# A two-block transformer kernel: weight splits of the delta net taken apart, and the end of each delta-net half reordered with the keys ahead of the queries

## Chip, cores and metric

The kernel runs on one core of a Trainium2 chip. The metric is device time in microseconds for one execution. PE is TensorE, DVE is VectorE, ACT is ScalarE, POOL is GpSimd, SP the queue engine that issues most DMAs.

## What is computed

Two transformer blocks follow each other on x of shape (1, 512, 1024), all in float32. The first has a differential attention, a gated delta net that runs forward and backward, a merge of both, and an expert-choice feed-forward layer with 16 experts; the second has a band attention, an RWKV layer and a feed-forward layer. The change lies in the first block alone. Its delta net, cut to what matters:

```python
qkv_g = jax.nn.silu(centred_depthwise_conv(qkv_g, conv_w[l]))      # 5 taps
qg, kg, vg = jnp.split(qkv_g, [GDN_QK, 2 * GDN_QK], axis=-1)        # 8 heads of 128
qg = l2norm(qg...); kg = l2norm(kg...)
g_f = -exp(a_log_fwd) * softplus(a_f + dt_bias_fwd)                 # and g_b
beta_f = sigmoid(b_f)                                               # and beta_b
# gated_delta_rule_chunked, forward and on flipped inputs:
q = chunks(q) * dk ** -0.5
g = jnp.cumsum(chunks(g), axis=-1)
decay = where(incl, exp(g_i - g_j), 0)
a_mat = where(strict, (k_beta @ k.T) * decay, 0)
sol = triangular_solve(a_mat + I, [v * beta, k_beta * exp(g)])
qk = where(incl, (q @ k.T) * decay, 0)
# then a scan over the chunks: o = q_dec @ S + qk @ v_new, S updated
```

## The kernel before

Everything is one program written out by hand for five engines that meet through counted semaphores. Each engine works strictly in the order written. Weights of the projections come through a ring of three slots. A weight tile is split into a rounded high part (`split_act`, L481, on ACT, 128x2048) and the remainder (`split_pool`, L489, on POOL, in place); PE then makes three products per 128 rows (L570 to L572). Split number k may be written once the tile of number k-2 has been used.

**Attention.** `attention_pe` projects queries, keys and values (L591 to L593), `attention_act` copies the value tiles out (L769). Between value projection and scores lie the small computations of the decays: ACT's L775, L776 and L778 (exponentials on 128x64) and DVE's L876 to L886. DVE's `maxima` (L892) reads the scores (L683), ACT's L785 makes the exponentials. At the end DVE scales the heads (L927), PE turns them (L727, `heads_out_pe`, behind the first delta-net tile), and ACT copies them (L822).

**Delta net.** It works in two halves of four heads (`gr` 0 and 1), each with three phases.

1. `group_*`: twelve feature tiles (4 queries, 4 keys, 4 values) are projected. Per tile ACT copies the projection twice (L1266 and, as the middle tap, L1274), DVE adds the other four taps (L1322) and forms the silu (L1309) with ACT's tanh (L1285), PE turns the tile to tokens (L1219), ACT copies it (L1288), POOL squares it (L1349) and DVE sums the squares (L1304). From tile 6 on ACT also makes one exponential of the decay matrices `DE` per tile (L1294, four instructions). After tile 11 come Ln and Exp of the norms (L1278, L1280), each with a table load. DVE scales eight token tiles (L1337), PE turns them back (L1253) into banks 4 and 5 by turns, ACT copies them (L1298).
2. `heads_*`: eight Gram products on PE (L1363: four key by key into banks 0 to 3, four key by query into banks 4 to 7). DVE multiplies the key products with the decays of each direction into `PT` (L1419), POOL multiplies these by beta (L1446), ACT copies the query products (L1392), POOL multiplies them by the decays (L1450). ACT copies the 16x16 corners of `PT` (L1095, eight per direction, named lanes f and b) into `C32`; DVE adds the two halves (L1135). Then the triangular systems are inverted: row matmuls (L1008), a chain of DVE steps (L1147, L1150), a widening (L1156), and so on. POOL makes masked copies `LT` (L1201).
3. `scan_*`: four chunks in each direction.

PE's waits at the end of a half, in its own order:

```python
            pe.wait_ge(*count("iv_sel", gr + 1))
            pe.wait_ge(*count("gd_pt", 8 * (gr + 1)))
            pe.wait_ge(*count("gd_qk", HG * (gr + 1)))
            for p in range(7 + 2):
                if p < 8:
                    inv_rows_pe(pe, f, gr, sel, p)
                if p >= 2:
                    inv_rows_pe(pe, b, gr, sel, p - 2)
```

## Time and profile before

| | |
|---|---|
| median of 3 runs | 2964.2 us (2950.64 to 2964.31) |
| profiled execution | 2965.58 us, span 2963.4 us |
| busy: PE, DVE, ACT, POOL | 90%, 31%, 26%, 20% |
| mean granted TensorE clock | 0.959 of 2.4 GHz |
| chain that ended last | PE 70%, DMA 12%, DVE 9%, ACT 5% |

The granted clock is 1.00 (2.4 GHz) or 0.50 (1.2 GHz) at any moment, and a mean over a stretch says how much of it was at either. In a timeline a row gives start, duration (of all instructions of the row), engine, line, operation, output and input, shape and count; in brackets stands how long the engine was idle ahead of it and what ended that. A matmul of float32 operands is shown as two instructions, a transpose as one.

### The profile page before, as it was taken

The page shows a single profiled execution, that of the slowest core. Times are in us where ns is not written, and L with a number is a line of the kernel's source. Part 1 is how long each engine was busy: PE and PEld are TensorE (multiplying, and loading weights), DVE is VectorE, ACT ScalarE, POOL GpSimd, SP SyncE. Part 2 cuts the span into 40 slices and gives each one's busy share as a digit, 9 for nine tenths or more (in the row PEclk, how much of TensorE's full clock was granted, in tenths as well). Part 3 has the DMA queues.
Part 4 walks back from the last instruction along what each step waited for, and adds up shares of the span by engine and source line. Part 5 has one row for each costly group of instructions (what it writes and reads, how often), then busy time and mean ns, then how long its engine had stood idle before and what let it go on. Part 6 is the DMA issues. An engine that isn't in the chain of part 4 may idle for free.

```text
span 2963.4 us, 34221 instructions
## 1 busy us (share of the span) xinstructions
PE 2661.8 (90%) x14439; PEld 1739.9 (59%) x14439; DVE 911.3 (31%) x1604; ACT 759.9 (26%) x1290; POOL 582.3 (20%) x173
## 2 busy tenths in 40 slices
PE   7989978879999999888988898888878899999998
PEld 5756767768566743323323333356657766788886
DVE  2348655654111311011011110123565521241221
ACT  3247643532111110000100100043342121431222
POOL 3310452452113000000000000022211122244442
PEclk9999979979999999999999999999988999999999
DMA  4300312203224699999999999943100032322322
GB/s 143 114 29 1 114 58 86 72 15 114 85 85 155 261 383 428 427 429 428 429 429 428 428 429 428 428 150 114 50 14 1 16 114 93 121 91 87 100 100 71
DMA packets 130852, 559.36 MB, mean 189 GB/s; under 512 B 7256, under 2 KB 88480, under 8 KB 103080
## 3 DMA queue, kind: packets, MB, share of 16 engines
q1 hardware_dynamic: 129864, 551.28, 46.8%
q0 software_dynamic: 864, 6.29, 0.5%
q8 instruction: 95, 1.56, 0.2%
q14 instruction: 29, 0.24, 0.0%
HBM read 547.01 MB, written 10.54 MB: 188 GB/s over the span
## 4 chain that ended last, share of the span: by engine, by line
PE 70%; DMA 12%; DVE 9%; ACT 5%; issue 2%; POOL 0%; DVEq 0%; SPq 0%; ACTq 0%; POOLq 0%
DMA S<-in_w_up 11%; PE PS L570 8%; PE PS L572 8%; PE PS L571 8%; PE PS L2101 7%; PE PS L2068 7%; PE PS L560 4%; PE PS L2051 2%; PE PS L3217 2%; PE PS L3219 2%; PE PS L3220 2%; PE PS L3064 2%; PE PS L2112 1%; DMA S<-in_w_down 1%; PE PS L548 1%
## 5 line engine op out<-in xcount | busy, mean ns | idle before, releaser
L2363 POOL TENSOR_TENSOR r_block<-S,r_block 128x2048 fp32r<-128x2048 f32 x57 | 261.5, 4588 | 1488.3 <-ACT r_block L2352 1479.5
L2068 PE MATMUL PS<-S 128*64 128x512 f32 x2048 | 458.3, 598 | 72.3 <-DMA S<-in_w_up 68.8
L570 PE MATMUL PS<-r_block,r_block 128*128 128x512 f32 x1040 | 417.8, 402 | 3.2 <-POOL r_block L2363 2.0
L572 PE MATMUL PS<-r_block,r_block 128*128 128x512 f32 x1040 | 405.3, 390 | 0.0
L571 PE MATMUL PS<-r_block,r_block 128*128 128x512 f32 x1040 | 404.8, 389 | 0.0
L2068 PEld LDWEIGHTS PS<-S 128*64 128x64 f32 x2048 | 141.3, 137 | 380.1 <-issue 248.4
L489 POOL TENSOR_TENSOR r_block<-S,r_block 128x2048 fp32r<-128x2048 f32 x40 | 183.1, 4578 | 565.4 <-ACT r_block L481 457.2
L2101 PE MATMUL PS<-S 128*64 128x512 f32 x1024 | 225.6, 597 | 5.8 <-DMA S<-in_w_down 2.5
L570 PEld LDWEIGHTS PS<-r_block,r_block 128*128 128x128 f32 x1040 | 195.3, 188 | 49.6 <-issue 8.0
L571 PEld LDWEIGHTS PS<-r_block,r_block 128*128 128x128 f32 x1040 | 195.4, 188 | 45.0 <-issue 6.0
L572 PEld LDWEIGHTS PS<-r_block,r_block 128*128 128x128 f32 x1040 | 195.2, 188 | 41.4
L2235 DVE SCALAR_TENSOR_TENSOR S<-S,PS 128x512 f32<-128x512 f32 x32 | 22.0, 688 | 486.2 <-ACT S L2163 462.8
L2101 PEld LDWEIGHTS PS<-S 128*64 128x64 f32 x1024 | 75.8, 138 | 144.7 <-issue 139.9
L2352 ACT ACTIVATE r_block<-S 128x2048 fp32r<-128x2048 f32 x57 | 108.9, 1912 | 171.8 <-PE PS L3220 117.6
L560 PE MATMUL PS<-S 128*128 128x512 f32 x256 | 110.5, 592 | 0.0
L3217 PE MATMUL PS<-r_block,r_block 128*128 128x512 f32 x256 | 99.8, 390 | 1.4 <-ACT S L3236 1.4
L481 ACT ACTIVATE r_block<-S 128x2048 fp32r<-128x2048 f32 x40 | 76.4, 1913 | 95.8 <-DMA S<-in_w_in 68.2
L2242 DVE TENSOR_TENSOR S<-S,PS 128x512 f32<-128x512 f32 x32 | 20.6, 684 | 258.6 <-PE PS L2068 258.6
L3219 PE MATMUL PS<-r_block,r_block 128*128 128x512 f32 x256 | 99.6, 389 | 0.0
L3220 PE MATMUL PS<-r_block,r_block 128*128 128x512 f32 x256 | 99.6, 389 | 0.0
L3259 DVE TENSOR_TENSOR S<-S 128x512 f32<-128x512 f32 x32 | 37.9, 1185 | 188.7 <-ACT S L3236 188.7
L1322 DVE SCALAR_TENSOR_TENSOR PS<-S,PS 128x512 f32<-128x512 f32 x96 | 72.5, 756 | 44.3 <-ACT PS L1274 41.7
(455 smaller groups left out, 3686.4 us busy)
## 6 DMA issues: line engine op xcount, KB each, us to landing
S<-in_w_gate SPq DMA_DIRECT2D x64, 2048.0 KB, 17.9
S<-in_w_up SPq DMA_DIRECT2D x64, 2048.0 KB, 21.0
S<-in_w_down SPq DMA_DIRECT2D x64, 2048.0 KB, 25.6
S<-in_w_in SPq DMA_DIRECT2D x57, 1024.0 KB, 5.1
S<-in_w_up SPq DMA_DIRECT2D x16, 1024.0 KB, 5.3
S<-in_w_down SPq DMA_DIRECT2D x16, 1024.0 KB, 4.8
S<-decay_rows SPq DMA_DIRECT2D x8, 1024.0 KB, 6.7
S<-in_w_out SPq DMA_DIRECT2D x8, 1024.0 KB, 4.9
```

The source lines that it names most:

```text
L489: pool.tensor_tensor(r32(w), w, rounded(WH[k % 2]), ALU.subtract).then_inc(sem("w_low"), 1)
L560: mm = pe.matmul(out, w[:, dc, off:off + P], src[:, dc, :], start=(dc == 0), stop=(dc == DC - 1))
L570: pe.matmul(out, wh, r32(HT[:, dc, :]), start=(dc == 0), stop=False)
L571: pe.matmul(out, wh, r32(low[:, dc, :]), start=False, stop=False)
L572: mm = pe.matmul(out, wl, r32(HT[:, dc, :]), start=False, stop=(dc == DC - 1))
L2068: mm = pe.matmul(PS[c * CAP:(c + 1) * CAP, 2 + 2 * m + g, :], XE[:, 2 * q + r, e * CAP:(e + 1) * CAP], w[:, r, 1024 * g + 512 * c:1024 * g ...
L2101: mm = pe.matmul(PS[c * CAP:(c + 1) * CAP, 6 + half, :], HE[e][:, f, :], w[:, f % 4, 512 * half:512 * half + 512], start=(f == 0), stop=(f ...
L2352: act.activation(r32(WH[k % 2]), slot2(name), ACT.Copy).then_inc(sem("w2_high"), 1)
L2363: pool.tensor_tensor(r32(w), w, rounded(WH[k % 2]), ALU.subtract).then_inc(sem("w2_low"), 1)
L3217: pe.matmul(PS[:, n, :], uh, r32(grid(wh.rearrange("p a b -> p (a b)"), 2)[:, f % 2, s]), start=first, stop=False)
L3219: pe.matmul(PS[:, n, :], uh, r32(wl[:, f % 2, s]), start=False, stop=False)
L3220: mm = pe.matmul(PS[:, n, :], ul, r32(grid(wh.rearrange("p a b -> p (a b)"), 2)[:, f % 2, s]), start=False, stop=last)
```

## The change

- **Splits.** ACT's rounding for the first delta-net weights goes ahead of the last four value copies, the one for the second weights behind the norms of attention. POOL's split of the second waits until DVE has scaled all heads.
- **Group phase.** The exponentials of the decays are made up to two per tile, and end at tile 10. POOL multiplies the forward decays by beta there (`DEB`, in the place of `OG`'s second half). DVE's two start copies go ahead of the last taps. Ln and Exp stand right behind the last tap copy.
- **End of a half.** DVE scales the four keys alone, PE turns them and makes the key products at once (banks 3 to 0); only then come the turns of the last two value tiles (now through banks 6 and 7), the four queries (scaled by POOL) and the query products. The forward `PT` is one product with `DEB` and needs no product by beta. The forward corners are shared: even ones on ACT, ahead of the query copies, odd ones on DVE.
- **SP** waits for all eight turns, not four, ahead of the decay rows.

```diff
         def attention_pool(pool):
-            for j in range(2):
-                split_pool(pool, ("g", 0, j))
+            split_pool(pool, ("g", 0, 0))
+            pool.wait_ge(*count("an_scaled", AH))
+            split_pool(pool, ("g", 0, 1))
         def attention_act(act):
-                split_act(act, after(("v", j)))
+                split_act(act, after(("v", j)) if j < 3 else ("g", 0, 0))
...
-            for j in range(2):
-                split_act(act, ("g", 0, j))
...
             act.activation(ors, oln, ACT.Exp, scale=-0.5).then_inc(sem("an_r"), 1)
+            split_act(act, ("g", 0, 1))
+        BACK = (7, 6, 5, 4, 0, 1, 2, 3)
+        DEB = OG[:, HG:2 * HG, :]
+        def inv_odd_corners_dve(dve, w, n):
+            for k in range(4):
+                q, s = quadrant(k), slice(32 * k + HALF, 32 * k + 2 * HALF)
+                dve.tensor_scalar(w["C32"][1][q].rearrange("p (u c) s -> p u c s", u=HG), units(w["PT"])[q, :, :, s],
+                                  const("par")[q, 1:2], None, ALU.mult).then_inc(sem(f"iv_c32_{w['l']}"), 1)
         def group_act(act, gr):
+                if j == 11:
                     act.wait_ge(*count("gn_ss", 8 * (gr + 1)))
                     act.activation(rnorm_l, rnorm, ACT.Ln, bias=eps).then_inc(sem("gn_ln"), 1)
...
-                if j >= 6:
-                    d, hl = divmod(j - 6, HG)
+                for d, hl in {6: ((0, 0),), 7: ((0, 1), (0, 2)), 8: ((0, 3),), 9: ((1, 0), (1, 1)), 10: ((1, 2), (1, 3))}.get(j, ()):
...
+            tanh(12 * gr + 11)
+            for i in range(HG):
+                turn_back(i)
+            for i in range(2):
+                act.wait_ge(*count("gt_turned", 12 * gr + 11 + i))
+                act.activation(TOK[:, 10 + i, :], PS[:, 6 + i, :], ACT.Copy).then_inc(sem("gt_copied"), 1)
+            for i in range(HG, 2 * HG):
+                turn_back(i)
         def group_dve(dve, gr):
             dve.wait_ge(*count("gn_r", gr + 1))
+            for i in range(HG):
+                t = grid(TOK[:, BACK[i], :], TC)
+                dve.tensor_tensor(t, t, spread(rnorm[:, BACK[i], :], P), ALU.mult).then_inc(sem("gn_scaled"), 1)
             dve.tensor_scalar(rnorm[:, 0:4, :], rnorm[:, 0:4, :], P ** -0.5, None, ALU.mult).then_inc(sem("gn_q"), 1)
+            silu(10)
+            silu(11)
         def group_pool(pool, gr):
+                if j == 6:
+                    for hl in range(HG):
+                        pool.wait_ge(*count("gd_decay", 8 * gr + hl + 1))
+                        pool.tensor_tensor(grid(DEB[:, hl, :], TC), grid(DE[0][:, hl, :], TC), beta_of(0, HG * gr + hl), ALU.mult)\
+                            .then_inc(sem("iv_pt0"), 1)
         def heads_pe(pe, gr):
+            turn_back_pe(pe, gr, range(HG))
+            pe.wait_ge(*count("gt_copied", 12 * gr + 10))
+            pe.wait_ge(*count("gp_copied", 24 * (gr + 1)))
+            for i in range(HG):
+                pe.wait_ge(*count("gn_back", 8 * gr + i + 1))
+                gram_pe(pe, HG - 1 - i, HG - 1 - i, HG)
+            for i in range(2):
+                pe.wait_ge(*count("gc_silu", 12 * gr + 11 + i))
+                for c in range(TC):
+                    mm = pe.transpose(PS[:, 6 + i, block_of(c)], RAW[:, 10 + i, block_of(c)], ident)
+                mm.then_inc(sem("gt_turned"), 1)
+            turn_back_pe(pe, gr, range(HG, 2 * HG))
             pe.wait_ge(*count("gn_back", 8 * (gr + 1)))
+            for hl in range(HG):
+                if hl == 2:
+                    pe.wait_ge(*count("gt_copied", 12 * (gr + 1)))
+                gram_pe(pe, HG + hl, hl, 0)
         def heads_act(act, gr):
+            act.wait_ge(*count("gd_pt", 8 * gr + 7))
+            inv_corners_act(act, f, gr, (0,))
             for hl in range(HG):
                 act.wait_ge(*count("gd_gram", 8 * gr + HG + hl + 1))
                 act.activation(QKD[0][:, hl, :], PS[:, HG + hl, :], ACT.Copy).then_inc(sem("gd_qk"), 1)
...
+            act.wait_ge(*count("iv_pt1", HG * (gr + 1)))
+            inv_corners_act(act, b, gr)
         def heads_dve(dve, gr):
+            for i in range(HG):
+                hl = HG - 1 - i
+                dve.wait_ge(*count("gd_gram", 8 * gr + i + 1))
+                dve.tensor_tensor(f["PT"][:, hl, :], PS[:, hl, :], DEB[:, hl, :], ALU.mult).then_inc(sem("gd_pt"), 1)
+                dve.tensor_tensor(b["PT"][:, hl, :], PS[:, hl, :], DE[1][:, hl, :], ALU.mult).then_inc(sem("gd_pt"), 1)
+            dve.wait_ge(*count("gd_pt", 8 * (gr + 1)))
+            inv_odd_corners_dve(dve, f, gr)
         def heads_pool(pool, gr):
+            pool.wait_ge(*count("gn_q", gr + 1))
+            pool.wait_ge(*count("gn_scaled", 8 * gr + HG))
+            for j in range(HG):
+                t = grid(TOK[:, j, :], TC)
+                pool.tensor_tensor(t, t, spread(rnorm[:, j, :], P), ALU.mult).then_inc(sem("gn_scaled"), 1)
+            for i in range(HG):
+                hl = HG - 1 - i
+                pool.wait_ge(*count("gd_pt", 8 * gr + 2 * i + 2))
+                t = grid(b["PT"][:, hl, :], TC)
+                pool.tensor_tensor(t, t, beta_of(1, HG * gr + hl), ALU.mult).then_inc(sem("iv_pt1"), 1)
         # SP
-                    sp.wait_ge(*count("gn_turned", 8 * gr + 4))
+                    sp.wait_ge(*count("gn_turned", 8 * (gr + 1)))
```

ACT at the end of the value projection, before (L481 a rounding, L769 the value copies, L775 to L778 the exponentials of the decays):

```order
L745 ACT_TABLE_LOAD
L745 ACTIVATE S<-S 128x64
L746 ACT_TABLE_LOAD
L746 ACTIVATE S<-S 128x64
L769 ACTIVATE S<-PS 128x512 x4
L481 ACTIVATE r_block_574<-S 128x2048
L481 ACTIVATE r_block_637<-S 128x2048
L775 ACTIVATE S<-S 128x64
```

and now (L770 the value copies, L773 the first of the exponentials):

```order
L746 ACT_TABLE_LOAD
L746 ACTIVATE S<-S 128x64
L747 ACT_TABLE_LOAD
L747 ACTIVATE S<-S 128x64
L481 ACTIVATE r_block_574<-S 128x2048
L770 ACTIVATE S<-PS 128x512 x4
L773 ACTIVATE S<-S 128x64
```

One rounding stands ahead of the copies, and none between them and the exponentials.

PE at the end of the first half's projection, before (L1219 turns to tokens, L1253 turns back, L1363 Gram products, L1008 row matmuls):

```order
L571 MATMUL PS<-r_block_78,r_block_637 128x512
L572 MATMUL PS<-r_block_593,r_block_695 128x512
L1219 MATMUL PS<-S 128x128 x12
L1253 MATMUL PS<-S 128x128 x32
L1363 MATMUL PS<-S 128x128 x32
L1008 MATMUL PS<-S 128x256 x29
```

and now (L1226 and L1401 turns to tokens, L1260 turns back, L1265 Gram products, L1009 row matmuls):

```order
L571 MATMUL PS<-r_block_78,r_block_637 128x512
L572 MATMUL PS<-r_block_593,r_block_695 128x512
L1226 MATMUL PS<-S 128x128 x4
L1260 MATMUL PS<-S 128x128 x16
L1265 MATMUL PS<-S 128x128 x16
L1401 MATMUL PS<-S 128x128 x8
L1260 MATMUL PS<-S 128x128 x16
L1265 MATMUL PS<-S 128x128 x16
L1009 MATMUL PS<-S 128x256 x29
```

The number of transposes and products is the same; half of the turns back and of the products stand ahead of the last two turns to tokens.

DVE at the same place, before (L1322 taps, L1309 silu, L1331 and L1337 scaling, L1130 start copies, L1419 products with the decays, L1135 the sum of the corners):

```order
L1322 SCALAR_TENSOR_TENSOR PS<-S,PS 128x512 x4
L1309 SCALAR_TENSOR_TENSOR S<-S,PS 128x512
L1331 TENSOR_SCALAR S<-S 128x16
L1337 TENSOR_TENSOR S<-S 128x512 x3
L1309 SCALAR_TENSOR_TENSOR S<-S,PS 128x512
L1337 TENSOR_TENSOR S<-S 128x512 x5
L1130 COPY S<-S 128x256 x2
L1419 TENSOR_TENSOR S<-PS,S 128x512 x8
L1135 TENSOR_TENSOR S<-S,PS 128x256
```

and now (L1348 taps, L1359 and L1360 scaling, L1332 silu, L1460 and L1461 products of the two directions, four of each by turns, L1133 odd corners, L1142 the sum):

```order
L1137 COPY S<-S 128x256 x2
L1348 SCALAR_TENSOR_TENSOR PS<-S,PS 128x512 x4
L1359 TENSOR_TENSOR S<-S 128x512 x4
L1360 TENSOR_SCALAR S<-S 128x16
L1332 SCALAR_TENSOR_TENSOR S<-S,PS 128x512 x2
L1460 TENSOR_TENSOR S<-PS,S 128x512
L1461 TENSOR_TENSOR S<-PS,S 128x512
...
L1133 TENSOR_SCALAR PS<-S 32x256 x4
L1142 TENSOR_TENSOR S<-S,PS 128x256
```

Four of the eight scalings are gone from DVE, the silus stand behind the other four, and four corner copies have come in.

## Rows read from the trace of the kernel before

**Rows 1.** ACT timeline, start of attention (start us, us, engine, line, operation, form, count)

```profile
180.61 3.70 ACT L481 ACTIVATE r_block<-S 128x2048 fp32r<-128x2048 f32 x2
184.21 0.24 ACT L775 ACTIVATE S<-S 128x64 f32<-128x64 f32 x1
```

**Rows 2.** POOL timeline, end of projection and start of attention

```profile
131.34 4.60 POOL L489 TENSOR_TENSOR r_block<-S,r_block 128x2048 fp32r<-128x2048 f32 x1 [8.36 <-ACT r_block L481]
...
182.59 8.96 POOL L489 TENSOR_TENSOR r_block<-S,r_block 128x2048 fp32r<-128x2048 f32 x2 [23.32 <-ACT r_block L481]
```

**Rows 3.** DVE timeline, the same stretches

```profile
131.84 4.65 DVE L842 TENSOR_TENSOR S<-S 128x512 f32<-128x512 f32 x1
...
182.26 0.29 DVE L882 TENSOR_TENSOR S<-S 128x32 f32<-128x32 f32 x2
184.49 2.67 DVE L885 TENSOR_SCALAR S<-S 128x64 f32<-128x64 f32 x1 [1.93 <-ACT S L775]
187.07 4.53 DVE L886 TENSOR_SCALAR S<-S 128x64 f32<-128x64 f32 x1
191.53 1.21 DVE L892 TENSOR_REDUCE S<-PS 128x2 f32<-128x1024 f32 x1
```

**Rows 4.** PE timeline, start of attention

```profile
181.58 1.99 PE L683 MATMUL PS<-S 64*128 64x512 f32 x8
...
194.47 2.08 PE L683 MATMUL PS<-S 64*128 64x512 f32 x4 [10.68 <-ACT S L785]
```

**Rows 5.** PE timeline, end of the first delta-net half

```profile
363.59 0.60 PE L1219 MATMUL PS<-S 128*128 128x128 f32 x4
...
376.59 5.36 PE L1253 MATMUL PS<-S 128*128 128x128 f32 x24 [0.72 <-ACT S L1298]
382.64 7.41 PE L1363 MATMUL PS<-S 128*128 128x128 f32 x64 [0.69 <-ACT S L1298]
395.30 4.56 PE L1008 MATMUL PS<-S 128*128 128x256 f32 x12 [5.25 <-DVE S L1135]
401.99 9.13 PE L1008 MATMUL PS<-S 128*128 128x256 f32 x32 [2.13 <-DVE S L1135]
```

**Rows 6.** PE timeline, end of the second half

```profile
568.20 0.60 PE L1219 MATMUL PS<-S 128*128 128x128 f32 x4
...
600.00 4.56 PE L1008 MATMUL PS<-S 128*128 128x256 f32 x12 [5.25 <-DVE S L1135]
```

**Rows 7.** ACT timeline, end of the first half

```profile
367.11 1.28 ACT L1278 ACT_TABLE_LOAD   x1
...
370.04 0.23 ACT L1280 ACTIVATE S<-S 128x32 f32<-128x32 f32 x1
...
390.76 0.51 ACT L1095 ACTIVATE S<-S 32x256 f32<-32x256 f32 x1
```

**Rows 8.** Stretches: PE, PEld, DVE, ACT, POOL busy, granted clock, DMA share, GB/s

```profile
184.00:186.00 2.00, 0.00 (x0) 0.00 (x0) 1.51 (x1) 0.74 (x4) 2.00 (x1) 1.00 0.00 0
...
380.00:382.00 2.00, 1.95 (x10) 1.28 (x8) 0.00 (x0) 1.33 (x4) 0.00 (x0) 0.62 1.03 418
...
398.00:400.00 2.00, 1.86 (x7) 1.01 (x5) 1.78 (x5) 1.95 (x3) 2.00 (x1) 0.86 0.00 0
...
405.00:456.00 51.00, 37.18 (x831) 32.84 (x831) 28.74 (x78) 15.22 (x23) 20.11 (x8) 0.70 0.01 2
```

**Rows 9.** POOL timeline, end of the first half

```profile
357.59 1.04 POOL L1349 TENSOR_TENSOR S<-S 128x512 f32<-128x512 f32 x1 [4.88 <-DVE S L1304]
...
384.68 8.09 POOL L1446 TENSOR_TENSOR S<-S 128x512 f32<-128x512 f32 x8 [24.20 <-DVE S L1419]
...
401.79 8.99 POOL L1201 TENSOR_TENSOR S<-S 128x2048 f32<-128x2048 f32 x2
```

**Rows 10.** DVE timeline, end of the first half

```profile
364.98 3.13 DVE L1322 SCALAR_TENSOR_TENSOR PS<-S,PS 128x512 f32<-128x512 f32 x4 [1.00 <-ACT PS L1274]
...
386.58 3.08 DVE L1419 TENSOR_TENSOR S<-PS,S 128x512 f32<-128x512 f32 x5 [0.20 <-PE PS L1363]
```

119 lines of the change are left out of this document (50 added, 69 removed).

## The prediction

> **What bounds the kernel now.** I read the page first: PE is busy 90% of the span, yet the change touches none of the big projections or expert matmuls, so its worth lies in stretches where PE stands still. The chain of waits names them: the start of attention (from 180.6 us) and the end of each delta-net half (363.6 to 395.3 and 568.2 to 600.0 us). There I read each engine's timeline, and the granted clock in short stretches.
>
> At the start of attention ACT does two weight roundings of 1.9 us each [rows 1]; the tiny exponential L775, for which DVE waits, starts only at 184.21. The roundings release two POOL splits (182.59, 8.96 us for both) [rows 2]. DVE's two products on 128x64, L885 and L886, then take 2.67 and 4.53 us, where both L882 together, on half the columns, take 0.29 [rows 3]. They end at 187.2 and 191.6, the middle and the end of the POOL pair. The first maximum (L892) starts at 191.53, though PE had made the scores by about 183 (eight instructions, 1.99 us from 181.58), and PE itself stands still 10.68 us [rows 4]. So most of this stretch is a wait for POOL.
>
> At the end of a half, PE's last transposes under the projection are at 363.59 and the first row matmul of the inversion (L1008) at 395.30: 31.7 us [rows 5]. The second half has 568.20 and 600.00: 31.8 [rows 6]. In between is one chain: taps, then Ln and Exp with their table loads on ACT (reached at 367.11, behind four exponentials of the decays) [rows 7], scaling on DVE, eight turns back of 0.9 us, eight Gram products of 0.9 us (7.41 for all) [rows 5], the copy of the last query product, eight corner copies on ACT of 0.5 us each from 390.76 [rows 7], the sum L1135, the rows.
>
> **The change, part by part.**
>
> *Splits.* The rounding of the first delta-net weights goes ahead of the last value copies. ACT is idle there, so its 1.9 us and POOL's 4.5 lie under PE's value tiles, and DVE has nothing to do then. The other rounding goes behind attention. L775 can then start beside the second L882, at about 182.4, and takes 0.24 [rows 1, 3]; L885 and L886 take 0.2 each; L892 starts at 182.85 instead of 191.53: **8.7 us**. Taking only ACT's 3.7 us away would not do it: POOL must be free. PE then waits about 2.4 us, not 10.68, for its next scores. The clock was still whole in the window that begins where PE stopped [rows 8] and half when it came back: four score instructions took 2.08 us where eight had taken 1.99 [rows 4]. I take it as staying whole and add **1.0**. The late rounding delays the head copies on ACT by the part of its 1.9 us that their wait for PE does not cover: **-0.4**. POOL's part of it waits for all head scalings, and ends about 2 us before PE wants it, behind the second tile. It may hold up one DVE memset, at most 4.6 us, of which the first tiles' slack hides all.
>
> *Work moved into the projection* (decay exponentials two per tile in places, four products by beta on POOL, two small copies on DVE) costs nothing: ACT waits for PE in every tile, and POOL has 4.88 idle us before its last square, which four products of 1.01 us just fit [rows 9]. If they did not, the Ln would be late by the excess. SP's wait for all eight turns puts the decay rows and the next two weight loads some 3 us later; they are wanted 10 us and more after they land.
>
> *The end of a half*, in the first half's times. ACT goes from the tap copy, after which DVE's taps start at 364.98 [rows 10], straight to the Ln: table load, Ln, table load, Exp take 367.11 to 370.27 now [rows 7], 3.16 us, so they end at 368.1, as do the taps. DVE scales four keys, about 0.63 us each: first done at 368.8. PE turns them back at 0.9 each, to 372.6, and makes the four key products, at half clock 1.8 each instead of 0.9. When does the clock rise? After 395.30, in dense row matmuls, it rose 3.3 us on; among the transposes from 373.06 only at about 381.5, 8.4 us on [rows 8]. From 372.6 the first gives 376, from 368.9 the second gives 377.3. I take 376: products end at 374.4, 376.2, 377.1, 378.0. DVE multiplies each twice at 0.62 [rows 10], to about 379.2, and the odd corners end by 381; POOL has scaled the four queries by 375. PE then turns the two value tiles (0.5 each) and the four queries, where ACT's copies set the pace, 0.6 each with six in a row; the last is copied at 382.15. The query products end at 385.8. ACT does four even corners (to 384.1) under them, copies the last product by 386.4, and the rows start at 386.45. Against 395.30: **8.85**. PE has then been idle under 1 us where it was idle 5.25 [rows 5]; it had fallen to half clock, and the first four row matmuls, 2.06 us of the chain, take about 1.15: **0.9**. The next wait, at 401.99, is 2.13 us and will be about 1.6; the eight instructions behind it took 3.7 at half clock and would take 2.3 at full. I take half of that: **0.7**. The sum is 10.45 per half, 20.9 for two.
>
> What is late next? The backward corners (ACT, 386.4 to 390.4) precede DVE's wish for them (392). POOL's two query products and two masks take 9.0 us a pair [rows 9] and end at 404.5.
>
> Here a rule is weighed. In the trace L842, a tensor_tensor with both inputs in SBUF, took 4.65 us beside a POOL split of 131.34 to 135.94, while L1419, of the same size but with one input in PSUM, keeps its 0.62 beside POOL's products by beta [rows 2, 3, 9, 10]. L1156 is of L842's kind; it would come at about 405.2, only 0.7 us behind the masks, where it has 5 us of air now. The Trainium skill, "SBUF — State Buffer", section "Who interferes with whom", says that a Vector instruction with two SBUF inputs contends with a GpSimd one that reads SBUF, the second to issue blocking fully, and that one with a single SBUF input outside the two-port modes is free. By that rule the corners into PSUM are free too and the sum stays, if the 0.7 us hold; rival 3 is the case in which they don't.
>
> **Sum:** 8.7 + 1.0 - 0.4 + 20.9 = 30.2 us. The profiled execution took 2965.58: 2935.4. The median of the three runs is 1.4 lower, so **2934.0**. Everything behind the second half starts earlier as a whole.
>
> **Bounds.** The start of attention gives 8.3 (the clock falls all the same) to 10.3. A half gives 6.3 if all key products, value turns and query turns run at half clock (rows at 389.9, plus the 0.9), and 12.5 if the clock is back by 374.5 and stays through the backward wait. Together 21 to 35 us. One of the three runs was 13.6 us below the others for no cause that this profile shows, and the new median could lie as far down.
>
> **Rivals.**
>
> 1. *The clock stays half through the query turns.* For it: transposes brought it back only after 8.4 us. Against: four dense products come between. Gain 21: 2943.
>
> 2. *The ends hardly move.* PE works in order, so value and query turns now sit behind the key products. If those came 9 us late, for POOL's products by beta or the moved exponentials, rows would start where they do now and only attention's 9 us would stay: 2955. Against: POOL has 0.8 us to spare, and DVE waits for PE, not POOL.
>
> 3. *L1156 runs into POOL's masks, in both halves.* If DVE is there 1 to 3 us before a mask ends, it waits that long (L842's mechanism), which takes back 2 to 6 us: 2938. The skill's page named above gives this as its rule for two SBUF inputs.
>
> 4. *Slower.* The early products, on a PE just out of an idle stretch, leave the clock at half through the whole inversion. Key products would end at 379.8, six turns at 385.4, query products at 392.9, rows start at 393.5: 1.8 won. From 405 to 456, where the mean clock is now 0.70 with PE busy 37 us [rows 8], two fifths of that work would double: 15 lost. Two halves cost 26, attention gives 9: 2981. It decides if no dense stretch lifts the clock; the row matmuls of now lifted it in 3.3 us.
>
> That the change does not do what it says can be put aside: the order shows each move.
>
> **How the numbers follow.** Differences under 0.5% (14.8 us) cannot be told from none here. Forecast (2929 to 2940): 0.57. Rival 3: 0.10. The same gains with a median 13 us further down (2921): 0.09. Rival 1 or part of it (2940 to 2947): 0.13. Rival 2: 0.09, two thirds of it above 2949.4. Rival 4: 0.02. The range 2919 to 2946 leaves out some 0.15. Faster by over 0.5%: 0.92; within 0.5%: 0.06; slower: 0.02.
>
> **What would show each step.** Products L885 and L886 (one line up in the new code) at 0.2 us; the first maximum at 182.9; four score instructions after it in 1.1. From the last projection transposes to the first inversion row 22.9 us (now 31.7); the Ln's table load 1.3 us after the last projection matmul; whole clock by 376 to 377. L1156 at 0.4 us each. Wrong if that distance is over 26 us, if L1156 takes longer than 1 us, if the clock from 376 to 386 reads 0.5, or if a stretch behind 700 us changes its length by more than 3 us.

## The result, and the profile after

The changed kernel takes 2932.6 us (median of 5 runs, 2927.4 to 2936.6), the kernel before beside it 2963.6 (median of 5, 2950.6 to 2964.3). The ratio is 0.9893 with a 95% interval of 0.988 to 0.9906: 31 us faster. The profiled execution took 2930.2 us with a span of 2928.4, against 2963.4 before: 35.0 us. PE still is busy 90% of the span (2646.6 us, 2661.8 before); the mean granted clock went from 0.959 to 0.968.

The two spans, cut at marks that both traces have:

| stretch | before | after | gain | predicted |
|---|---|---|---|---|
| start to last value copy | 180.12 | 181.34 | -1.2 | 0 |
| last value copy to Exp of attention's norms | 111.32 | 101.34 | 10.0 | 9.7 |
| to the last transposes under the first projection | 72.15 | 72.28 | -0.1 | -0.4 |
| to the first row matmul, half 0 | 31.71 | 21.21 | 10.5 | 8.85 |
| to the scan | 56.94 | 54.61 | 2.3 | 1.6 |
| scan and second projection | 115.96 | 115.37 | 0.6 | 0 |
| to the first row matmul, half 1 | 31.80 | 21.19 | 10.6 | 8.85 |
| to the scan | 57.08 | 54.77 | 2.3 | 1.6 |
| all behind it | 2306.32 | 2306.29 | 0.0 | 0 |

The table is in us. "Start to last value copy" ends where ACT copies the last value tile; the marks behind it are starts of instructions too. The 1.2 us lost ahead of attention are none of the change's: the first 64 transposes took 9.99 us in this execution and 8.90 in the other. Nor can the 2.3 us "to the scan" be put down to the change alone: in the run e1_splits below, which keeps both ends as before, the first half needs 54.45 us there and the second 56.90, and the other runs without fillers, e7 aside, lie between 54.2 and 58.9. What the traces show different between them is where the clock fell.

**Start of attention.** Rows of the DVE, POOL, PE and ACT timelines of the changed kernel, one engine after the other:

```profile
183.78 0.20 DVE L884 TENSOR_SCALAR S<-S 128x64 f32<-128x64 f32 x1
183.89 0.19 DVE L885 TENSOR_SCALAR S<-S 128x64 f32<-128x64 f32 x1
184.05 1.22 DVE L891 TENSOR_REDUCE S<-PS 128x2 f32<-128x1024 f32 x1
...
172.52 4.60 POOL L489 TENSOR_TENSOR r_block<-S,r_block 128x2048 fp32r<-128x2048 f32 x1 [11.98 <-ACT r_block L481]
289.22 4.59 POOL L489 TENSOR_TENSOR r_block<-S,r_block 128x2048 fp32r<-128x2048 f32 x1 [112.10 <-DVE S L926]
...
187.01 1.13 PE L683 MATMUL PS<-S 64*128 64x512 f32 x4 [1.99 <-ACT S L783]
...
181.34 0.60 ACT L770 ACTIVATE S<-PS 128x512 f32<-128x512 f32 x1 [2.12 <-PE PS L593]
```

The two products that took 2.67 and 4.53 us [rows 3] take 0.20 and 0.19, because the POOL split that lay beside them [rows 2] now ends at 177.1. From the last value copy to the first maximum are 2.71 us; before they were 11.41. PE stands still 1.99 us, not 10.68, and its next four scores take 1.13, not 2.08 [rows 4]: the clock stayed whole.

**End of the first half.** PE timeline of the changed kernel (L1226 turns to tokens, L1260 turns back, L1265 Gram products, L1401 the two value tiles, L1009 rows):

```profile
354.96 0.60 PE L1226 MATMUL PS<-S 128*128 128x128 f32 x4
360.27 3.61 PE L1260 MATMUL PS<-S 128*128 128x128 f32 x16 [4.71 <-DVE S L1359]
363.71 3.74 PE L1265 MATMUL PS<-S 128*128 128x128 f32 x32
367.28 1.04 PE L1401 MATMUL PS<-S 128*128 128x128 f32 x8
...
369.64 1.12 PE L1260 MATMUL PS<-S 128*128 128x128 f32 x8 [0.45 <-ACT S L1278]
371.44 3.84 PE L1265 MATMUL PS<-S 128*128 128x128 f32 x32 [0.69 <-ACT S L1278]
376.17 1.97 PE L1009 MATMUL PS<-S 128*128 128x256 f32 x8 [0.89 <-ACT S L1437]
...
381.91 7.47 PE L1009 MATMUL PS<-S 128*128 128x256 f32 x32 [2.12 <-DVE S L1142]
```

ACT in the same stretch (L1300 and L1302 Ln and Exp of the norms, L1278 copies of the turns back, L1437 of the query products):

```profile
356.33 1.28 ACT L1300 ACT_TABLE_LOAD   x1
...
359.26 0.23 ACT L1302 ACTIVATE S<-S 128x32 f32<-128x32 f32 x1
...
370.30 1.09 ACT L1278 ACTIVATE S<-PS 128x512 f32<-128x512 f32 x2 [0.32 <-PE PS L1260]
...
375.32 0.60 ACT L1437 ACTIVATE S<-PS 128x512 f32<-128x512 f32 x1 [0.30 <-PE PS L1265]
```

And DVE (L1460 the first product with the decays, L1133 the odd corners, L1163 the widening):

```profile
364.90 0.69 DVE L1460 TENSOR_TENSOR S<-PS,S 128x512 f32<-128x512 f32 x1 [1.61 <-PE PS L1265]
...
369.81 2.03 DVE L1133 TENSOR_SCALAR PS<-S 32x256 f32<-32x256 f32 x4
...
393.84 0.88 DVE L1163 TENSOR_TENSOR S<-S 128x256 f32<-128x256 f32 x2
```

Against [rows 5] the one long chain has become two beside each other: DVE's products and corners, done at 371.8, and the turns of the queries, whose copies on ACT end at 371.4. Behind them come ACT's even corners, the query copies and the rows. The clock of the changed kernel in stretches (PE, PEld, DVE, ACT, POOL busy, granted clock, DMA share, GB/s):

```profile
360.00:362.00 2.00, 1.73 (x8) 1.57 (x8) 2.00 (x5) 1.53 (x3) 0.00 (x0) 0.52 0.00 0
362.00:364.00 2.00, 2.00 (x13) 1.73 (x12) 1.29 (x4) 1.30 (x4) 1.82 (x2) 0.62 0.00 0
364.00:366.00 2.00, 2.00 (x20) 2.00 (x20) 1.10 (x2) 0.51 (x1) 2.00 (x3) 1.00 0.03 8
380.00:382.00 2.00, 0.09 (x1) 0.09 (x1) 1.83 (x6) 2.00 (x2) 2.00 (x2) 1.00 1.08 347
...
406.00:408.00 2.00, 1.65 (x124) 1.54 (x115) 1.51 (x4) 0.00 (x0) 2.00 (x1) 0.50 0.03 8
```

It was half for the key turns only (it fell at 360.1, just ahead of the first, and was back at 363.5, before the first product), whole for all products, and it outlived the backward wait at 380, the 2.1 us that PE stands still before the first rows of the backward lane. Before, it fell in this wait, and the next row matmuls ran at half clock, as this stretch of the kernel before shows:

```profile
402.00:404.00 2.00, 2.00 (x5) 1.64 (x6) 0.50 (x2) 0.54 (x1) 2.00 (x1) 0.50 0.03 8
```

### The profile page after: what moved, and what is told of

It is laid out like the page before. It is cut to its first block, busy times and chain, and to the rows that moved or that the text cites. A ratio compares the mean times of both kernels' runs of the same rounds, so it can differ in the third digit from the quotient of the medians.

```text
span 2928.4 us, 34208 instructions
## 1 busy us (share of the span) xinstructions
PE 2646.6 (90%) x14439; PEld 1730.9 (59%) x14439; DVE 902.9 (31%) x1604; ACT 755.7 (26%) x1282; POOL 591.1 (20%) x181
## 4 chain that ended last, share of the span: by engine, by line
PE 71%; DMA 13%; DVE 9%; ACT 4%; issue 2%; POOL 0%; DVEq 0%; SPq 0%; ACTq 0%; POOLq 0%
DMA S<-in_w_up 11%; PE PS L570 8%; PE PS L572 8%; PE PS L571 8%; PE PS L2149 7%; PE PS L2116 7%; PE PS L560 4%; PE PS L2099 2%; PE PS L3265 2%; PE PS L3267 2%; PE PS L3268 2%; PE PS L3112 2%; PE PS L2160 1%; DMA S<-in_w_down 1%; PE PS L548 1%
## 5 line engine op out<-in xcount | busy, mean ns | idle before, releaser
L481 ACT ACTIVATE r_block<-S 128x2048 fp32r<-128x2048 f32 x40 | 76.5, 1912 | 100.2 <-DMA S<-in_w_in 68.8
L1348 DVE SCALAR_TENSOR_TENSOR PS<-S,PS 128x512 f32<-128x512 f32 x96 | 72.5, 756 | 43.1 <-ACT PS L1296 40.5
## 6 DMA issues: line engine op xcount, KB each, us to landing
S<-in_w_down SPq DMA_DIRECT2D x64, 2048.0 KB, 25.6
```

## The experiments

All are made from the kernel before or from the changed kernel. Medians stand against 2932.6 of the changed kernel and against runs of the kernel before taken beside each group (2964.4 to 2965.5). "Distance" is the time from the last transposes under the projection to the first row matmul, in half 0 and half 1; the changed kernel has 21.21 and 21.19.

### The two parts apart

**e1_splits**, the kernel before with:

```diff
-            for j in range(2):
-                split_pool(pool, ("g", 0, j))
+            split_pool(pool, ("g", 0, 0))
+            pool.wait_ge(*count("an_scaled", AH))
+            split_pool(pool, ("g", 0, 1))
...
-                split_act(act, after(("v", j)))
+                split_act(act, after(("v", j)) if j < 3 else ("g", 0, 0))
...
+            split_act(act, ("g", 0, 1))
```

> The kernel before with the change of the splits alone (ACT's first rounding ahead of the last value copies, its second behind the norms, POOL's second split behind all head scalings); both ends of a half stay as they were. If the POOL split was what held the two products on 128x64, they take 0.2 us each, the first maximum starts 8.7 us earlier against the last value copy, the next score instructions keep the whole clock, and the end of attention is 10 us earlier against the same mark: a median 9 to 10 us under before, 2954. Rival (the gain of the whole change came from the ends, the splits only shift a wait to the tail of attention): the maximum is early, but the norms' end is less than 5 us early, and the median is within 5 us of before.

Measured: 2956.6, ratio 0.9972 (0.9963 to 0.9981), 8 us, where 9 to 10 were expected. From the last value copy to the norms' Exp it is 101.30 us, as in the changed kernel; the ends keep 32.02 and 31.65.

**e2_ends**, the changed kernel with those lines as before.

> The changed kernel with the splits put back as before (both ACT roundings behind the value copies, POOL's behind them at once). If the parts add, the start of attention is as before (products of 2.7 and 4.5 us, first maximum 8.7 us later than in the changed kernel), and each half keeps 10.5 us to its first row matmul and 2.3 us in the inversion: 25.6 us, a median of 2938. Rival (the two parts lean on one another, as the late second split frees ACT and POOL for the first tiles): a half gains 1 us or more less than in the changed kernel.

Measured: 2943.1, ratio 0.9925 (0.9912 to 0.9939), 21.6 us. Attention is at 110.97, distances 21.32 and 21.92. The parts add: 8.0 and 21.6 are 29.6, together they gave 31.0. The second half missed the expectation, with 58.01 us from rows to scan instead of 54.8, and by its length alone it meets the sign of the rival (1 us or more less gained). Its rows show the late clock described below and no other difference.

### What held DVE

**e3_pool_held**, the changed kernel with one wait more:

```diff
+            pool.wait_ge(*count("ab_gc", 1))
             split_pool(pool, ("g", 0, 0))
```

> The changed kernel with one added wait: POOL's split of the first delta-net weights starts only when the last running sums are copied (the semaphore that also releases the small exponential), so that it lies beside the two products on 128x64 again, while ACT's roundings stay where the change put them. If POOL's hold on DVE made the stretch long, the products are held for up to 4.5 us, the first maximum is 3 to 4.5 us later than in the changed kernel, and the median is 3 to 5 us above it, 2936 to 2938. Rival (ACT's two roundings of 3.7 us ahead of the exponential were the cause, POOL's length only happened to match): the products take 0.2 us, the maximum starts as in the changed kernel, 2932.6.

Measured: 2939.6, ratio 0.9917 (0.9902 to 0.9932), 7 us above the changed kernel, more than the 3 to 5 expected. DVE's timeline of this run:

```profile
182.32 4.60 DVE L882 TENSOR_TENSOR S<-S 128x32 f32<-128x32 f32 x2
186.85 0.18 DVE L885 TENSOR_SCALAR S<-S 128x64 f32<-128x64 f32 x1
...
187.05 1.21 DVE L892 TENSOR_REDUCE S<-PS 128x2 f32<-128x1024 f32 x1
```

and POOL's beside it:

```profile
182.37 4.50 POOL L489 TENSOR_TENSOR r_block<-S,r_block 128x2048 fp32r<-128x2048 f32 x1 [23.04 <-DVE S L879]
```

The hold is there, with ACT's roundings out of the way, but one step ahead of the place I had named: the subtractions on 128x32, 0.29 us otherwise, caught it, and the products found POOL done. The maximum came 4.2 us later, and then the scores ran at half clock again (2.08 us behind 6.14 idle): attention took 106.42, 5.1 more. POOL's split alone is enough to hold DVE, so the rival, in which POOL's length only happened to match, is out. How the 8.7 us divide between the two is not shown: no run keeps ACT's roundings and moves POOL away. The medians are close, and the two intervals just touch (0.9902 here, 0.9906 for the changed kernel); the finding rests on the rows.

**e7_masks_late**, the changed kernel with POOL's masks pushed back:

```diff
+            pool.wait_ge(*count("iv_step0", 31 * gr + 25))
             for w in (f, b):
                 inv_lt_pool(pool, w, gr)
```

> The changed kernel with POOL's two masked copies held until DVE has done twelve of the fifteen forward steps, so that they run about 390.3 to 399.3 us, across DVE's widening products, two instructions of 0.4 us each with two SBUF inputs, and beside the steps of the inversion, which have one input in PSUM. If a DVE instruction with two SBUF inputs is held while POOL works on SBUF, one of the two widening products takes about 4.5 us, the steps beside it keep their 0.2 to 0.3 us, and a half loses 4 to 5 us: a median of 2941. Rival (the hold of the start of attention is a matter of that place, of POOL's split or the small shapes, and not of the two SBUF inputs): the widening products stay at 0.4 us each, and the masks are ready in time for PE: no more than 1 us lost.

Measured: 2943.8, ratio 0.9937 (0.9921 to 0.9954), 11 us above the changed kernel. DVE's timeline in its first half (L1154 and L1157 the steps, L1163 the widening):

```profile
392.87 0.26 DVE L1154 TENSOR_TENSOR PS<-PS,S 128x96 f32<-128x96 f32 x1
393.16 0.25 DVE L1157 TENSOR_TENSOR S<-S,PS 128x96 f32<-128x96 f32 x1
...
393.96 6.00 DVE L1163 TENSOR_TENSOR S<-S 128x256 f32<-128x256 f32 x2
```

and POOL's two masks:

```profile
390.52 9.15 POOL L1208 TENSOR_TENSOR S<-S 128x2048 f32<-128x2048 f32 x2 [5.41 <-DVE S L1157]
```

In the midst of the masks the steps with an input in PSUM keep 0.25 us; the pair with both inputs in SBUF takes 6.00 instead of 0.76, and rows to scan grew from 54.6 to 60.9 (62.9 in the other half). This is rival 3 of the prediction, provoked. In the changed kernel itself the pair takes 0.88, and the masks end at 394.1: a graze of 0.1 us.

### The parts of a half's end, taken back one at a time

**e4_late_norm**: exponentials of the decays one per tile, two of them and Ln, Exp behind the loop.

```diff
-                if j == 11:
-                    act.wait_ge(*count("gn_ss", 8 * (gr + 1)))
-                    act.activation(rnorm_l, rnorm, ACT.Ln, bias=eps).then_inc(sem("gn_ln"), 1)
...
-                for d, hl in {6: ((0, 0),), 7: ((0, 1), (0, 2)), 8: ((0, 3),), 9: ((1, 0), (1, 1)), 10: ((1, 2), (1, 3))}.get(j, ()):
+                for d, hl in {6: ((0, 0),), 7: ((0, 1),), 8: ((0, 2),), 9: ((0, 3),), 10: ((1, 0),), 11: ((1, 1),)}.get(j, ()):
...
+            act.wait_ge(*count("gn_ss", 8 * (gr + 1)))
+            act.activation(rnorm_l, rnorm, ACT.Ln, bias=eps).then_inc(sem("gn_ln"), 1)
...
             tanh(12 * gr + 11)
+            for d, hl in ((1, 2), (1, 3)):
...
```

> The changed kernel with the exponentials of the decays at one per tile as before, so that two of them come behind tile 11, and Ln and Exp of the norms behind the last of the loop's work. PE's wait ahead of the key turns grows from 4.7 to about 7.5 us. Theory A (the clock comes back 3.3 us after the turns start, since they and the key products then follow each other without a gap, however long PE stood still before): the clock is whole again at the same distance from the first turn, rows start about 2.8 us later per half, and the median is 6 to 7 us above the changed kernel, 2939. Theory B (the short wait is what let the clock come back early; behind a wait of 7 us and more it takes 8 us, as before the change): the key products run at half clock, 1.8 us each, rows start 6 us later per half, and the median is 12 us or more above, 2945.

Measured: 2940.6, ratio 0.9919 (0.9904 to 0.9935), 8 us above, between the two. Distances 25.57 and 25.06, 4.4 and 3.9 more. PE's timeline of this run:

```profile
362.58 1.97 PE L1260 MATMUL PS<-S 128*128 128x128 f32 x8 [6.86 <-DVE S L1363]
365.24 1.94 PE L1260 MATMUL PS<-S 128*128 128x128 f32 x8 [0.70 <-ACT S L1278]
366.98 4.99 PE L1265 MATMUL PS<-S 128*128 128x128 f32 x32
```

and the clock in it (columns as above):

```profile
366.00:368.00 2.00, 2.00 (x11) 2.00 (x10) 0.00 (x0) 1.19 (x2) 2.00 (x3) 0.50 0.04 8
368.00:370.00 2.00, 2.00 (x13) 2.00 (x12) 0.97 (x2) 0.00 (x0) 0.52 (x1) 0.60 0.00 0
```

PE waits 2.15 us longer, a gap of 0.70 appears between the turns since ACT copies late behind its exponentials, and the clock comes back at 369.6, 7 us behind the first turn instead of 3.2; the products take 4.99 instead of 3.74. Theory A's fixed distance is wrong, and so is B's half clock through all products. So of the 4.4 us only 2.15 are the longer wait; the rest goes through the gap and the clock.

**e5_corners_act** (odd corners on ACT), **e6_queries_dve** (queries scaled on DVE), one run each:

```diff
-            inv_corners_act(act, f, gr, (0,))
+            inv_corners_act(act, f, gr)
...
-            inv_odd_corners_dve(dve, f, gr)
```

> The changed kernel with all eight forward corners on ACT again (four more copies of 0.5 us ahead of the query copies) and none on DVE. If ACT is the engine that ends the chain to the first row matmul, the last query copy and the first row come 1.9 to 2.1 us later per half: 23.2 us from the last transposes under the projection to the first row, instead of 21.2, a time 4 us up, about 2936. Rival (the chain goes through DVE's eight products and its own four corners of 0.5 us each, so that taking them off DVE gives back what ACT loses): the distance stays within 0.5 us of 21.2.

Measured: 22.45 and 23.81; 1.2 and 2.6 more, 2933.4 in the one run. Less than ACT's 2.0 in the first half, since the last query copy no longer waits for PE. In the second half the clock came back late (6.0 us behind the first turn instead of 2.9), which is in the 2.6.

and for the queries, in `heads_pool` and behind `silu(11)`:

```diff
-                pool.tensor_tensor(t, t, spread(rnorm[:, j, :], P), ALU.mult).then_inc(sem("gn_scaled"), 1)
...
+                dve.tensor_tensor(t, t, spread(rnorm[:, j, :], P), ALU.mult).then_inc(sem("gn_scaled"), 1)
```

> The changed kernel with the four queries scaled on DVE, behind the two silus, instead of on POOL. DVE's products would start when its scalings end, about 0.9 us later than the first key product allows; if DVE's products are on the chain, the distance from the last transposes under the projection to the first row grows by 0.9 us per half, to 22.1, and the time by 2 us. Rival (the key products on PE set the pace and DVE has air): the distance stays 21.2, and the POOL part of the change was worth nothing.

Measured: 21.32 and 21.06, no change (2930.8 in the one run): the rival holds. In the changed kernel ACT does its even corners only when the query turns are copied (371.4), while DVE's seventh product is done by 369.2; DVE has 2 us of air.

**e11_no_deb**: `DEB` gone, forward products with `DE[0]`, POOL multiplies them by beta.

```diff
-                dve.tensor_tensor(f["PT"][:, hl, :], PS[:, hl, :], DEB[:, hl, :], ALU.mult)
+                dve.tensor_tensor(f["PT"][:, hl, :], PS[:, hl, :], DE[0][:, hl, :], ALU.mult)
...
+                pool.wait_ge(*count("gd_pt", 8 * gr + 2 * i + 1))
+                t = grid(f["PT"][:, hl, :], TC)
+                pool.tensor_tensor(t, t, beta_of(0, HG * gr + hl), ALU.mult).then_inc(sem("iv_pt0"), 1)
```

> The changed kernel without the decays times beta computed in the projection: the forward products are made with the bare decays, and POOL multiplies each by beta, by turns with the backward ones, eight products of 1.03 us on the way to the corners. If that part is worth something, the forward corners start when POOL's seventh product ends, 1.6 us later, and the distance to the first row is 22.8 us instead of 21.2: 3 us up, 2936. Rival (the query products and their copies end the chain anyway): 21.2, the same time.

Measured: 2935.7, ratio 0.99 (0.9884 to 0.9917), 3 us up, which these intervals do not tell from the changed kernel; distances 23.16 and 23.29, 2.0 and 2.1 more, where its place on the chain said 1.6. In both halves the clock came back late here (5.2 and 6.0 us behind the first turn); the four key products of the first half took 4.46 us instead of 3.74, so the part itself is worth less than 2.0. POOL's seventh product and ACT's even corners of this run:

```profile
372.79 1.04 POOL L1489 TENSOR_TENSOR S<-S 128x512 f32<-128x512 f32 x1
...
373.87 2.10 ACT L1096 ACTIVATE S<-S 32x256 f32<-32x256 f32 x4 [1.37 <-POOL S L1489]
```

**e12_keys_late**: PE makes the key products behind all eight turns.

```diff
-            for i in range(HG):
-                pe.wait_ge(*count("gn_back", 8 * gr + i + 1))
-                gram_pe(pe, HG - 1 - i, HG - 1 - i, HG)
...
             turn_back_pe(pe, gr, range(HG, 2 * HG))
+            for i in range(HG):
+                pe.wait_ge(*count("gn_back", 8 * gr + i + 1))
+                gram_pe(pe, HG - 1 - i, HG - 1 - i, HG)
```

> The changed kernel with the four key products back behind all eight turns, as before the change, everything else as changed (early norms, forward beta in the projection, shared corners). If the order of PE is the main part of the gain at the end of a half, the distance to the first row goes back by most of the 10.5 us: 28 us or more, a median of 2946 or more. Rival, and what the trace gives step by step (queries turned back and copied by 367.8, key products to 371.4, DVE's products to 374, corners to 376.4, query copies to 378): 23 to 24 us, as long as the clock comes back during the turns, and a median of 2937 to 2939; most of the gain is then that of the early norms, of the forward beta and of the shared corners.

Measured: 2932.7, ratio 0.989 (0.9874 to 0.9907), as the changed kernel. Distances 22.03 and 23.28, 0.8 and 2.1 more. ACT of this run, the last two query copies and the even corners:

```profile
366.61 1.09 ACT L1278 ACTIVATE S<-PS 128x512 f32<-128x512 f32 x2 [0.32 <-PE PS L1260]
372.41 2.10 ACT L1096 ACTIVATE S<-S 32x256 f32<-32x256 f32 x4 [4.71 <-DVE S L1460]
```

In the first half that is even less than the rival gave, in the second it is what the rival gave (23 to 24); the median is below its 2937. Queries are then copied 3.7 us earlier, DVE's products end later, and the query products follow the key products without a gap; the two chains have changed places. The second half's 2.1 has a late clock in it (6.1 us behind the first turn, against 3.2 in the first half). "Keys ahead of the queries", the part after which the change is named, is the smallest but one.

The first-half prices, 4.4 for the early norms, 2.0 for beta in the projection, 1.2 for the shared corners, 0.8 for the keys and 0 for POOL's queries, make 8.4 of the 10.5. They are no clean sum: the first two were taken with the clock back late and the others with it back early, as in the changed kernel, and a late clock by itself costs 0.6 to 1.2 us of distance (below). What is left over may belong to parts that lean on one another; pairs were not run.

### A version with the clock held up

**e8_warm**, matmuls that nobody reads, 128x256 into free bank halves, in PE's waits:

```diff
+        def keep_upper(pe, bank, n):
+            for _ in range(n):
+                pe.matmul(PS[:, bank, 256:512], ident, const("mask4")[:, 0:256], start=True, stop=True)
...
+                    keep_upper(pe, 5, 10)
                 pe.wait_ge(*count("gn_scaled", 8 * gr + i + 1))
...
+            keep_upper(pe, 3, 3)
             inv_u4_pe(pe, f, gr)
             inv_rows_pe(pe, b, gr, sel, 7)
+            keep_upper(pe, 3, 4)
             inv_u4_pe(pe, b, gr)
...
```

> The changed kernel with matmuls without use of their results, 128x256 into free halves of banks, on PE where it stands still: ten ahead of the key turns (PE waits 4.7 us there), and 3, 4, 2, 2, 3, 3 ahead of the small products of the inversion. Theory (idle stretches, not the small products themselves, take the clock down): the clock stays whole, the key turns take 0.45 instead of 0.9 us each and the first row comes 1 us earlier, the small products from 396 to 418 us, now at half clock, take half the time and the scan starts 5 us earlier: a median of 2920. Rival (the clock falls among the small products whatever fills the waits): 1 us per half from the turns, and the fillers at half clock lengthen the waits, so that the median stays within 4 us of 2932.6.

Measured: 2929.1, ratio 0.9886 (0.987 to 0.9903), not the 2920 expected. The turns kept the whole clock: distances 20.30 and 20.27, 0.9 less each. The second group of 64x32 products took 2.06 us, not 3.62. But in the first half the clock fell among the 32x16 products all the same, while in the second it stayed whole through all 256 of them (595.7 to 601.4) and fell at 602.1, as the stretches of this run show:

```profile
402.00:404.00 2.00, 0.96 (x87) 0.84 (x87) 0.69 (x1) 0.59 (x1) 1.76 (x2) 1.00 0.00 0
404.00:406.00 2.00, 2.00 (x70) 1.78 (x62) 1.21 (x3) 0.00 (x0) 2.00 (x1) 0.54 0.04 8
...
598.00:600.00 2.00, 1.94 (x106) 1.46 (x106) 1.87 (x5) 0.00 (x0) 2.00 (x1) 1.00 0.03 8
600.00:602.00 2.00, 0.90 (x72) 0.90 (x74) 0.87 (x3) 0.00 (x0) 2.00 (x2) 1.00 0.00 0
602.00:604.00 2.00, 2.00 (x34) 1.63 (x26) 1.90 (x4) 1.32 (x3) 2.00 (x1) 0.53 0.04 8
```

The profiled execution of this run took 2922.9 us, 7.3 less than that of the changed kernel. That is not the fillers' doing: 7.5 us of it lie behind the second scan, where there are none (see the end of the next section).

**e9_trim** has only the fillers that seemed to pay: the 10 ahead of the key turns, and the 3 and 4 ahead of the two groups of 64x32 products.

> The kernel with fillers, less those behind the first small products: ten ahead of the key turns, 3 and 4 ahead of the two groups of 64x32 products, none later, where the clock fell to half all the same and the fillers took twice their time. If the fillers before them are what pays, each half keeps 0.9 us at its first row and 1.5 us at the second group of 64x32 products (2.1 instead of 3.6), and loses nothing behind: 53.0 us from the first row to the scan, instead of 54.6, and 4 to 5 us under the changed kernel, 2928. Rival (the clock of the products behind is a matter of chance and gives back or takes 2 us per half, whatever stands ahead): the median cannot be told from 2932.6.

Measured: 2928.3, ratio 0.9887 (0.9869 to 0.9904). Distances 20.27 and 20.28, but rows to scan 56.58 and 55.09, more than the 54.61 and 54.77 without fillers. The 1.5 us of the small products were given back: in half 0 the clock fell at 402.5 instead of 397.6 and then was still half for the last products (3.68 us, where the changed kernel has 2.08), and in half 1 it fell in the backward wait, at 573.2. This is the rival's outcome.

**e10_start** adds five fillers ahead of the first transposes, with a wait for the constants.

> The kernel e9_trim with five fillers more, ahead of the very first transposes, on constants that have landed by then; PE stands still there until 20 us, and the 64 transposes behind take 9 to 10 us, the first 3 to 6 us of them at 6 to 7 transposes per us, the others at 11. If the clock is whole when they start they take 6 us, and everything behind comes 2.5 to 3.5 us earlier, as far as the first weight split on POOL (26.3 us) allows: 2 to 3 us under e9_trim. Rival (the stage waits for that split or for the copies by other engines): the first projection matmul stays at 28.6 to 29.9 us, and the time is that of e9_trim.

Measured: 2928.4, ratio 0.9879 (0.9862 to 0.9895). PE's timeline of its start (L1256 the fillers, L551 the transposes, L573 the projection):

```profile
15.58 4.63 PE L1256 MATMUL PS<-S 128*128 128x256 f32 x10 [15.58 <-DMA S<-in_shape_constants]
20.00 7.97 PE L551 MATMUL PS<-S 128*128 128x128 f32 x64
27.73 0.48 PE L573 MATMUL PS<-r_block,r_block 128*128 128x512 f32 x1
```

The first projection matmul comes at 27.73, against 28.6 to 30.3 in the other runs. That is 0.9 to 2.6 us, and mostly less than expected, since the clock came back only 1 to 2 us into the transposes. Of the 2 to 3 us that this was to give against e9_trim the median shows nothing; in the profiled execution the clock fell in the backward wait of both halves (379.8 and 574.3). The three versions lie 3.5 to 4.3 us under the changed kernel by median, and their intervals overlap its own (0.988 to 0.9906): clearly faster than the kernel before, not told apart from the change.

## Why the prediction was right

2934.0 was forecast with a range of 2919 to 2946, and it became 2932.6; faster was right. Main mechanism and size hold, but that it came so close is partly luck: the stages of the profiled pair gained 35.0 us, not 30.2, because the ends of the halves were mis-sized by 3.4 and the rows behind them by 1.4, and the medians gained only 31.0. Point by point:

- **Splits, 8.7 us.** Right: 11.41 and 2.71 us from value copy to first maximum, 8.70. That POOL had to be free, and not only ACT, is shown by e3, on the subtractions one step ahead of the products. The Trainium skill, "SBUF — State Buffer", section "Who interferes with whom", has it so: two SBUF inputs on DVE against a GpSimd instruction that reads SBUF, the later one fully held; by that rule, e3 (4.60 us for 0.29) and e7 (6.00 for 0.76) agree, and so do the steps with a PSUM input, which e7 left at 0.25 us. The products of before have one input; for `tensor_scalar` the same section says that it can enter a two-port mode, which contends too, when its operands meet conditions. No row shows the mode; the 2.67 and 4.53 us, each ending with one of POOL's two splits, agree with it, and where POOL's split was elsewhere (e1, e3) the same products took 0.2.
- **Scores at whole clock, 1.0; late rounding, -0.4.** 0.95 for the first four score instructions by PE's rows, 1.3 in all (from these scores to the norms' Exp), since the clock of before stayed half until 200.6; the rounding cost 0.1.
- **First row of a half, 8.85.** Mis-sized; it was 10.5. The steps, with the predicted ones moved by 8.63 us (363.59 to 354.96):

| step, half 0 | predicted | measured |
|---|---|---|
| Exp of the norms ends | 359.5 | 359.5 |
| keys turned | 364.0 | 363.9 |
| clock whole | 367.4 | 363.5 |
| last key product ends | 369.4 | 367.4 |
| odd corners end | 372.4 | 371.8 |
| last query turned back copied | 373.5 | 371.4 |
| last query product copied | 377.8 | 375.9 |
| first row | 377.8 | 376.2 |

  The step that failed is "From 372.6 the first gives 376, from 368.9 the second gives 377.3. I take 376". I counted the dense work from the first key product. But the four key turns, 0.9 us each without a gap, were dense work too; before, the turns had gaps of 0.72 us and of several us between them [rows 5]. The clock rose 3.2 us after the first turn, while PE had done nothing but turns since its wait; the first half of e12, where only transposes follow for the next microseconds too, has the same 3.2.
- **Is that the clock's rule or luck?** In eight halves with this same end (the changed kernel, e2, e3, e7) it was whole 3.2 to 3.8 us after the first turn in five, and 4.7 to 5.9 us after it in three, with nothing different in PE's queue. Those three have distances of 21.9 to 22.5 instead of 21.2 to 21.4. The profiled execution had the early case twice; the forecast of 22.9 us is near the late case (22.4 in e3), so its miss of 1.6 us is in part chance. What tells the two cases apart is when the clock had fallen in the 4.71 us of idle time ahead of the turns. In the five early halves it fell between 0.2 us ahead of the first turn and 0.4 behind it, in the three late ones 1.0 to 2.1 us ahead. The eight halves of e5, e6, e11 and e12, with the same idle time, fit: fell at most 0.5 us ahead, back after 2.9 to 3.5 us (four halves); fell 0.8 to 1.7 ahead, back after 5.2 to 6.1 (four). What sets the moment of the fall is not shown. A late half, from e3 (PE's turns and key products, then clock stretches as above):

```profile
553.50 3.83 PE L1261 MATMUL PS<-S 128*128 128x128 f32 x16 [4.71 <-DVE S L1360]
557.13 4.72 PE L1266 MATMUL PS<-S 128*128 128x128 f32 x32
...
552.00:554.00 2.00, 0.50 (x3) 0.50 (x4) 1.96 (x4) 1.99 (x5) 0.00 (x0) 0.59 0.00 0
558.00:560.00 2.00, 2.00 (x14) 2.00 (x14) 0.82 (x2) 0.00 (x0) 1.46 (x2) 0.71 0.00 0
```

The Trainium skill, "TensorE: Matmul & The Clock Gate", section "What's actually happening", says that the same kernel can see the clock come back at other places from run to run, since the hardware looks at a free-running stretch of activity, and gives 500 ns either way. The eight halves agree that it varies, but their spread of 2.7 us is wider.
- **Backward wait, 0.7 ("I take half").** The halving was right on average and for no half: with the clock back early, it stayed whole through the wait of 2.1 us in five of five, with the clock late it fell in three of three. That is no rule for other versions: in the first halves of e5 and e12 it was back after 2.9 and 3.2 us and fell by this wait all the same, and in e8 to e10, where fillers had kept it whole, it fell in it or just behind it in four of six halves. Eight row matmuls of before's 3.7 us take 2.0 where it stays. That fits the difference of 2.3 and 1.6 us in the table of stages, but the 54.45 us of e1's first half, without this change, show that the difference is the clock's and not surely the change's. Distance and rows to scan together, a half with a late clock costs 2.5 to 4 us (e3: 22.37 and 56.03; e2: 21.92 and 58.01). That is a likely part of why the medians gained less than the profiled pair; unprofiled runs have no stages, so it is not shown.
- **Rival 3, the widening in the masks.** The 0.7 us of air had shrunk to nothing as the rows came earlier still, yet it cost only 0.1 us. e7 shows what 3 us more would have done.
- **Rivals 1, 2 and 4.** Clock half through the query turns: no run shows it. Ends that hardly move: no. The clock half through the inversion: it was whole until 397.6.
- **"What would show each step".** 0.2 us for the products, 1.1 for the scores, the Ln's table load 1.4 us behind the start of the last transposes (354.96 to 356.33): as said. 22.9 us became 21.2. Behind 700 us nothing changed: 2306.3 from the second scan to the end, twice.

The stretch behind the second scan, which no version touches, takes 2302.8 to 2306.5 us in the runs without fillers and 2298.8, 2300.2 and 2306.4 in e8, e9 and e10. Set side by side matmul by matmul, the executions part by more than 1 us at three places only: from 950 to 1000 us (router and start of the expert layer), from 1900 to 2070 (its end and the band attention), and by 1.2 to 1.3 us in some runs near 2160. The granted clock parts at the two large ones too. In the changed kernel it is 0.86 in the first and 0.85 from 2000 to 2070; in e8, whose times are 7 us lower there, 0.93 in both:

```profile
2000.00:2070.00 70.00, 53.06 (x334) 35.48 (x333) 38.01 (x80) 32.32 (x86) 2.34 (x1) 0.85 0.05 16
...
1993.00:2063.00 70.00, 52.12 (x344) 35.69 (x343) 38.00 (x80) 32.90 (x87) 4.22 (x1) 0.93 0.08 27
```

So up to 7.5 us between two executions of one program are the clock in stages that nobody changed, as much as most of the single prices above; those are read from the stages for this reason. Why the clock falls there in some executions stays open.

## What to carry to other kernels

A short DVE instruction that takes microseconds beside a POOL instruction is held, and the cure is to move POOL's work to where DVE waits anyway, not to speed up the engine that feeds it. When a chain is cut, price each part by taking it back alone: here the early start of two tiny activations was worth about 4 us a half, the clock's part included, and the reordering of the matmuls 0.8 to 2.1. Read such prices from the stage, and compare the clock in it first: a single price can hold 1 us and more of clock. Where PE restarts from an idle stretch, count all its gapless work towards the return of the clock, transposes too, and keep both outcomes in the range.

## What the runs showed of the hardware that I had not expected

- Once down, the clock's return varies from execution to execution: 2.9 to 6.1 us after the first turn at one and the same place. It came late where the clock had fallen 0.8 us or more ahead of the turns. In e4, where it had fallen 3.2 and 4.4 us ahead and a gap of 0.7 us stood among the turns, it took 7.0 and 5.9; which of the two did it is not shown.
- Float32 transposes alone bring the clock back: in the changed kernel it rose at 363.5, and PE's first product after the wait starts at 363.71.
- Dense fillers in the waits do not surely hold the clock through 256 products of 32x16: in e8 it fell among them at about 404.2, with waits of 0.4 and 1.0 us alone in the 7 us before, and stayed whole through them in the other half. Holding it before them only moved the half-clock stretch to later work (e9).
- The clock can fall with PE never idle for more than about 2 us: in the second half of e9 it had been whole since the projection and fell at 573.2, in a wait of 2.12 us behind shorter ones of 0.9 and 0.5.
- A held DVE pair can lose more than one POOL instruction: L1163 lost 5.2 us to two masks of 4.6 each, the rest of the first and nearly all of the second.
- In the first microseconds of the program the granted clock reads 1.00 while 4 to 5 transposes start per us, and 9 later (in the changed kernel from about 25.6 us on). The column cannot be trusted before its first change, the instruction rate can. (The 6 to 7 and 11 in the expectation of e10 are counts of one-microsecond stretches, in which an instruction that crosses an edge counts twice.)
